# Small buffers between the high and low halves of the operand buffers, in a two-block transformer kernel on one core

## What is computed

```python
def swiglu(u, w_in, w_out):
    a, b = jnp.split(u @ w_in, 2, axis=-1)
    return (jax.nn.silu(a) * b) @ w_out

u = modulate(rmsnorm(h, g_norm_ffn1[l]), sh1, sc1)
h = h + 0.5 * gt1 * swiglu(u, w_ffn1_in[l], w_ffn1_out[l])
...
x_lat = ffn_sublayer(x_lat, m_lat[0], m_lat[1], m_lat[2],
                     ffn_w_in[i, 0], ffn_w_out[i, 0], ln_g[i, 0], ln_b[i, 0])
```

## Time and profile before

| | us |
|---|---|
| median of 3 runs | 2530.74 |
| lowest, highest | 2529.84, 2531.62 |
| the profiled execution | 2532.03 |
| its span, from the first to the last instruction | 2530.2 |
| TensorE matmuls busy | 2445.1 |
| TensorE weight loads busy (beside the matmuls) | 2226.9 |
| VectorE busy | 1801.1 |
| ScalarE busy | 1106.5 |

### The profile page before, as it was taken

The page is one execution under the profiler, slowest core; times in us unless marked ns, Lnnn a source line. Parts: engine busy times, 40 slices in busy tenths (PEclk is TensorE's granted clock), DMA queues, the critical chain, the costliest instruction groups (busy, mean ns, idle before and its releaser), DMA issues.

```text
span 2530.2 us, 39280 instructions
## 1 busy us (share of the span) xinstructions
PE 2445.1 (97%) x15654; PEld 2226.9 (88%) x15654; DVE 1801.1 (71%) x3467; ACT 1106.5 (44%) x1656; POOL 0.2 (0%) x4
## 2 busy tenths in 40 slices
PE   4998999999999999999999999999999999998998
PEld 3998989999999888788888998888998888988997
DVE  7888887788977446768877669897785344676555
ACT  3444565544463324724223662232562222566443
POOL 0000000000000000000000000000000000000000
PEclk8999999999999999999999999999999999999999
DMA  8997656769855431653543256676374333122653
GB/s 317 334 332 266 211 193 191 250 234 313 304 196 188 140 100 59 208 159 125 154 141 121 85 183 202 192 237 199 119 241 148 94 125 95 62 92 91 202 185 99
DMA packets 161671, 454.72 MB, mean 180 GB/s; under 512 B 17745, under 2 KB 21329, under 8 KB 161489
## 3 DMA queue, kind: packets, MB, share of 16 engines
q1 hardware_dynamic: 161488, 452.21, 54.3%
HBM read 451.09 MB, written 1.05 MB: 179 GB/s over the span
## 4 chain that ended last, share of the span: by engine, by line
PE 77%; DVE 4%; ACT 4%; issue 1%; DMA 0%; ACTq 0%; DVEq 0%; SPq 0%
PE PS L1297 24%; PE PS L1299 24%; PE PS L1298 24%; DVE own L1803 1%; PE PS L1457 1%; PE PS L1324 1%; PE PS L1322 1%; ACT own L1525 1%; ACT Uh L1588 1%; PE PS L1506 1%; ACT NT L1592 1%; DVE X L1784 1%; PE PS L1489 0%; DVE X L1899 0%; ACT spare L1525 0%
## 5 line engine op out<-in xcount | busy, mean ns | idle before, releaser
L1297 PE MATMUL PS<-Uh,own 128*128 128x256 f32 (+1 forms) x2080 | 655.1, 315 | 30.4 <-DVE Ul L1888 21.7
L1298 PE MATMUL PS<-Ul,own 128*128 128x256 f32 (+1 forms) x2080 | 646.6, 311 | 0.0
L1299 PE MATMUL PS<-Uh,own 128*128 128x256 f32 (+1 forms) x2080 | 646.4, 311 | 0.0
L1525 ACT ACTIVATE own<-raw 128x1024 fp32r<-128x1024 f32 x425 | 443.3, 1054 | 360.9 <-PE PS L1299 298.6
L1803 DVE TENSOR_TENSOR own<-raw,own 128x1024 fp32r<-128x1024 f32 x425 | 515.0, 1220 | 76.6 <-ACT own L1525 76.2
L1297 PEld LDWEIGHTS PS<-Uh,own 128*128 128x128 f32 x2080 | 401.5, 193 | 55.4 <-issue 29.5
L1298 PEld LDWEIGHTS PS<-Ul,own 128*128 128x128 f32 x2080 | 401.8, 193 | 19.8 <-issue 0.2
L1299 PEld LDWEIGHTS PS<-Uh,own 128*128 128x128 f32 x2080 | 401.6, 193 | 19.7
L1297 PE MATMUL PS<-Hh,own 128*128 128x256 f32 (+1 forms) x1088 | 345.2, 317 | 0.0
L1298 PE MATMUL PS<-Hl,own 128*128 128x256 f32 (+1 forms) x1088 | 340.9, 313 | 0.0
L1299 PE MATMUL PS<-Hh,own 128*128 128x256 f32 (+1 forms) x1088 | 340.9, 313 | 0.0
(11 more groups left out here) (233 smaller groups left out, 3866.6 us busy)
## 6 DMA issues: line engine op xcount, KB each, us to landing
MODS<-in_mm SPq DMA_DIRECT2D x168, 256.0 KB, 3.8
SCR<-in_mm SPq DMA_DIRECT2D x136, 256.0 KB, 4.3
raw<-in_f0i SPq DMA_DIRECT2D x68, 512.0 KB, 4.2
raw<-in_f1i SPq DMA_DIRECT2D x56, 512.0 KB, 3.6
raw<-in_f2i SPq DMA_DIRECT2D x56, 512.0 KB, 3.6
SCR<-in_ma SPq DMA_DIRECT2D x88, 256.0 KB, 5.3
raw<-in_w1i SPq DMA_DIRECT2D x44, 512.0 KB, 5.4
raw<-in_w2i SPq DMA_DIRECT2D x44, 512.0 KB, 5.4
```

The lines of the kernel that those rows point to most:

```text
L1297: e.matmul(o, ll, rh, start=start, stop=False, skip_group_check=shared)
L1298: e.matmul(o, lh, rl, start=False, stop=False, skip_group_check=shared)
L1299: return e.matmul(o, lh, rh, start=False, stop=stop, skip_group_check=shared)
L1525: e.activation(parts(w.n)[0], raw[:, w.n % RING, :], ACT.Copy).then_inc(s["whi"].tell(w.n), 1)
```

## The change

The allocation of ones moves between those of Uh and Ul, and that of M between those of Hh and Hl. No size and no instruction is changed, and the order of the instructions on each engine is the same as before. raw, own, X and Uh keep their places. ones starts at byte 86144, Ul at 86656, Hh at 103040, M at 119424, Hl at 120864, SCR at 157728 and MODS at 222688. The buffers from Hl to V all move by 1952 bytes. The distance from Uh to Ul becomes 16896 bytes, that from Hh to Hl 17824.

```diff
@@ -1092,8 +1092,10 @@
         own = sb("own", [P, RING, 2048], F32R)
         X = sb("X", [P, KT, 512])
         Uh = sb("Uh", [P, KT, 512], F32R)
+        ones = sb("ones", [P, P])
         Ul = sb("Ul", [P, KT, 512], F32R)
         Hh = sb("Hh", [P, 2 * FS, 512], F32R)
+        M = sb("M", [P, 5 * 72])
         Hl = sb("Hl", [P, 2 * FS, 512], F32R)
         SA = sb("SA", [P, 2, 512])
         GT = sb("GT", [P, 2, 512])
@@ -1108,10 +1110,8 @@
             pass
         GW = sb("GW", [P, 3072])
         V = sb("V", [P, NV])
-        M = sb("M", [P, 5 * 72])
         CF = sb("CF", [P, 60 * 8])
         MODS = sb("MODS", [P, 1024])
-        ones = sb("ones", [P, P])
         ident = sb("ident", [P, P])
         small = sb("small", [P, 224])
         T2 = sb("T2", [P, P])
```

## The result

The change makes the kernel slower by 0.44%: 2542.86 us against 2531.18 (medians of four executions each), a ratio of 1.0044 with a 95% interval of 1.003 to 1.0057. The forecast was 2530.7 with a range that ended at 2534.0.

The account below looks back on a forecast made before the run. TensorE's row of matmuls was taken as the bound, busy 2445.1 of 2530.2 us. All terms (matmuls, VectorE and ScalarE, transfers, constants) were 0, so the median of three runs, 2530.74, gave 2530.7 us; range 2527.4 to 2534.0.

Parts of the forecast that it names:

- What bounds the kernel: TensorE's row of matmuls, busy 2445.1 of 2530.2 us; only 85 us of the span are free of matmuls.
- The matmuls that read the moved buffers get 0: Matmuls on lines 1297 to 1299: equal steps and durations across buffers, so new places cost 0 us.
- the argument of the pace: Matmul steps of 0.121 us (256 columns) and 0.227 (512): the fixed 0.015 us doesn't grow with columns, so no clash.
- faster: the fixed cost is the clash: Matmuls of three lines: halves clashed, costing 15 ns on each of 14736; up to 221 us won, 2310 us; chance 0.03.
- The rival "slower": Line 1298: new places clash with weights loaded from own or spare; 1 ns on 4912 matmuls, 4.9 us, 2535.6; chance 0.04.
- line 1298 beside 1299: Forecast is wrong if line 1298's mean differs from unmoved line 1299's by over 1 ns, same shape and clock moment.
- the zeros of VectorE: VectorE's splitting steps and fused products: durations stay, such as 420 ns and 747 ns, so 0 us.
- transfers into SCR: DMA into SCR at an odd multiple of 32 bytes: 0, bounded by 5% or 2.2 us either way.
- ones and M as buffers of their own: Constants moved between the halves: matrix loads with ones take 191 ns, as those with Hh and own, so 0.
- the untouched waits at the start: TensorE's two start-up waits of 20.2 and 17.1 us stay at 20 and 17 us within 2 us.
- the rule on starts at multiples of 256 bytes: DMA descriptors starting off such multiples fetch extra 32-byte beats; for writes into SCR, 64 + 4 before, 64 + 1 after.

Follow-up runs that it names:

- the sweep: Matmul groups behind the end of the kernel before, other engines idle, starts of weights and operands moved: 113.4 to 122.0 ns on 256 columns, 226.7 to 236.8 on 512.
- ones alone: The kernel before with only ones moved between Uh and Ul, M staying in place: 2532.16 against 2531.66 us, ratio 1.0004.
- gaps of 256: The changed kernel with M 96 bytes longer, so the gaps are 512 and 1536 bytes: 2530.76 against 2530.53 us, ratio 1.0000.
- a shift of 64 and 192 bytes: The kernel before with split weights of 256-column products in own starting 64 (high) and 192 bytes (low) further on: 2499.20 against 2530.53 us, ratio 0.9876.
- the halves 192 bytes on: The kernel before with 192 unused bytes ahead of Uh and 64 behind Hl: 2522.01 us, ratio 0.9949, executions from 2513.39 to 2531.49.

## Why the prediction was wrong

What bounds the kernel was right, and it is why the error matters: each nanosecond of a matmul is paid 14736 times.

The step that failed is "The matmuls that read the moved buffers get 0". Its rows are true, and they don't test what they were used for. All four halves, own, spare and spare_gw stood at the same distance modulo 256 before the change; the four slots of the ring and the blocks of 512 bytes within a slot are multiples of 256 apart as well. I read equal durations over many addresses as "places don't matter", while one and the same distance was measured again and again. The exact multiples were in the text (16384), as the thing that might be special between the halves; that it held between weights and operands, and that the new starts were no multiples of 256 from own any more, wasn't followed up. What stood in the place of that 0 is +16.5 us on 512 columns and -7.2 on 256.

The second failing step is the argument of the pace. "A clash between two streams inside the memory would be paid with each element read": the sweep shows a cost that takes the place of the constant part. At 256 columns the 13 ns above the streaming (120.0 less 256 columns at 2.4 a nanosecond, 106.7) become 7 at the best distance; at 512 they stay 13 at best and become 20 at 64 bytes, 23 at the worst combination. So the rival "faster: the fixed cost is the clash", given 0.03, had a true part; it was not the distance between the halves, and the change won only 7.2 us of it, beside a larger loss.

The rival "slower" had the place (the operand streamed beside weights being loaded) and the right sign, with 0.04 and 1 ns as its price. The measured price is 5 to 7 ns a matmul in 871 triples of 512 columns, against which stands a gain in those of 256. It was held to be unlikely for the reason that "Uh, Ul, Hh and Hl stream beside four slots ... at different distances now", which is false modulo 256. Its mark, line 1298 beside 1299, was a poor one too. It did show with Ul, Uh and spare (399 ns on line 1298, 392 on line 1299), but not with Hl, Hh and own (393 and 394), where 4.6 us were lost: line 1299 lengthened there from 389 to 394 ns although neither Hh nor own moved against each other modulo 256. The pace is that of a triple as a whole.

By the Trainium skill (TensorE: Matmul & The Clock Gate, Step-by-step: what each phase is for) "Loading the next tile's weights doesn't steal SBUF read bandwidth from the running matmul", by two independent read ports. No run here can see ports, and none has matmuls without a weight load of their own; but with the other engines idle the pace on 256 columns lay between 113.4 and 122.0 ns with nothing but the starts of weights and operands changed, so for fp32r products the measurement decides against taking the sentence as "without any effect".

Right were the zeros of VectorE (420, 747 ns), of transfers into SCR (3.7 us at either place), of ones and M as buffers of their own (the runs with ones alone and with gaps of 256), and the untouched waits at the start. Right too was to give no weight, on the written side, to the rule on starts at multiples of 256 bytes that the prediction takes from the Trainium skill (DMA: Bandwidth & Descriptors, How a descriptor splits into AXI transactions): SCR landed in 3.7 us at 128 and at 32 bytes past such a multiple.

What is left open: why the distance acts as it does, whether it is the weights of the running matmul or those loaded beside it for the next one that count, and what decides between two paces at one distance beyond the pace of the group ahead.

## What to carry to other kernels

When durations agree over many addresses, ask first which differences between these addresses occur at all: a layout in round sizes makes one and the same case out of them. A small tensor put between large ones moves everything behind it; keep its size a multiple of 256 bytes, or place it last, unless the new distance from weights to operands has been measured. Where a row of short fp32r matmuls bounds the time, the distance is worth a sweep: here 1.2% for a shift of 64 and 192 bytes. In such a sweep leave out the first ten matmuls of each group, and repeat a distance behind different ones.

## What was not expected of the hardware

The pace of a 128x128 fp32r matmul with its own weight load depends on the distance from the weights' start to the operand's start in a partition, modulo 256 bytes: 113.4 to 122.0 ns with 256 columns, 226.7 to 236.8 with 512, and what is best for one width is among the worst for the other (64 bytes: 113.4 and 233.5). It takes up to ten matmuls behind others with another distance before the steps repeat. At some distances two paces exist for the same instructions: 353 and 340 ns for three matmuls on 256 columns, 233.5 and 226.7 ns for one on 512 at 16 bytes. In the kernel with the halves 192 bytes on, executions spread by 18 us instead of 2 to 6; that the two paces do it is argued, not shown.
